# Norm factors by Ln and Exp on ScalarE, and the group norm's sums of squares placed behind the memory value tiles

## What is computed

```python
def rms_norm(x, g):
    xf = x.astype(jnp.float32)
    y = xf * lax.rsqrt(jnp.mean(xf * xf, axis=-1, keepdims=True) + RMS_EPS)
    return (y * g.astype(jnp.float32)).astype(x.dtype)
...
    # in rwkv7_mixer, after the recurrence; H = 16 heads of N = 64 channels
    mean = jnp.mean(y, axis=-1, keepdims=True)
    var = jnp.mean(jnp.square(y - mean), axis=-1, keepdims=True)
    yn = ((y - mean) * lax.rsqrt(var + RWKV_GN_EPS)).reshape(B, S, D)
    yn = yn * gn_g.astype(jnp.float32) + gn_b.astype(jnp.float32)
...
    out = (yn + bonus.reshape(B, S, D)).astype(x.dtype)
    return (out * g) @ w_o
```

## Time and profile before

| | |
|---|---|
| three runs | 3185.61, 3197.8, 3207.39 us; median 3197.8 |
| the profiled execution | 3202.03 us, of which span 3200.0 |
| mean granted clock of PE in it | 0.97 of full speed |
| PE busy | 3048.5 us, 16020 matmul records |
| DVE busy | 1005.6 us |
| ACT busy | 1026.7 us |
| POOL busy | 789.7 us |

### The profile page before, as it was taken

How to read it: one execution, slowest core, us unless ns; L and a number is a source line. 1 busy time by engine, 2 the same in 40 slices (tenths; PEclk the granted TensorE clock), 3 DMA queues, 4 the chain that set the end, 5 groups by cost and what they waited for, 6 DMA issues and landing times.

```text
span 3200.0 us, 37773 instructions
## 1 busy us (share of the span) xinstructions
PE 3048.5 (95%) x16020; PEld 2148.2 (67%) x16020; DVE 1005.6 (31%) x1552; ACT 1026.7 (32%) x1630; POOL 789.7 (25%) x399
## 2 busy tenths in 40 slices
PE   8999999999987999899999999998999999999996
PEld 6687778885675787577788777776887473333332
DVE  5444330115587743632411224144120330000001
ACT  4543442334662222243433324413221131111111
POOL 3122244441330000032344432200442121111110
PEclk9999999999898799999999999999999999999998
DMA  3242122230220002221232232110332249999996
GB/s 126 89 138 73 53 91 94 92 105 22 94 68 1 2 2 80 86 79 61 85 105 92 92 95 90 53 53 1 98 100 73 88 187 400 399 400 399 399 394 244
DMA packets 214262, 416.41 MB, mean 130 GB/s; under 512 B 18486, under 2 KB 195670, under 8 KB 201168
## 3 DMA queue, kind: packets, MB, share of 16 engines
q1 hardware_dynamic: 199248, 394.30, 33.8%
q0 software_dynamic: 14704, 19.70, 1.8%
q10 hardware_dynamic: 144, 0.01, 0.0%
HBM read 501.70 MB, written 16.79 MB: 162 GB/s over the span
## 4 chain that ended last, share of the span: by engine, by line
PE 86%; DVE 7%; ACT 3%; DMA 2%; issue 1%; POOL 1%; SPq 0%; ACTq 0%; POOLq 0%; DVEq 0%
PE product_banks L600 15%; PE product_banks L602 14%; PE product_banks L601 14%; PE product_banks L2227 10%; PE product_banks L2264 5%; PE product_banks L568 5%; PE product_banks L695 3%; PE score_banks L1203 1%; PE stat_bank L823 1%; PE product_banks L1224 1%; PE product_banks L976 1%; PE product_banks L2820 1%; DVE SC L751 1%; PE product_banks L1590 1%; PE stat_bank L733 1%
## 5 line engine op out<-in xcount | busy, mean ns | idle before, releaser
L500 POOL TENSOR_TENSOR Wr_parts<-Wr,Wr_parts 128x1024 fp32r<-128x1024 f32 x202 | 488.6, 2420 | 1138.1 <-ACT Wr_parts L477 1138.1
L601 PE MATMUL product_banks<-A_parts,Wr_parts 128*128 128x512 f32 x1520 | 594.4, 391 | 0.0
L477 ACT ACTIVATE Wr_parts<-Wr 128x1024 fp32r<-128x1024 f32 x202 | 213.4, 1059 | 633.4 <-PE product_banks L602 586.9
L2227 PE MATMUL product_banks<-A,Wr 128*64 128x512 f32 x1312 | 340.5, 597 | 1.2 <-ACT Wr L2290 1.2
L600 PE MATMUL product_banks<-H_parts,Wr_parts 128*128 128x512 f32 x840 | 334.5, 398 | 3.0 <-POOL Wr_parts L500 2.5
L602 PE MATMUL product_banks<-H_parts,Wr_parts 128*128 128x512 f32 x840 | 329.0, 392 | 0.0
L601 PEld LDWEIGHTS product_banks<-A_parts,Wr_parts 128*128 128x128 f32 x1520 | 287.2, 189 | 59.8 <-issue 1.0
L500 POOL TENSOR_TENSOR shared_con_parts<-Wr,shared_con_parts 128x1024 fp32r<-128x1024 f32 x80 | 192.1, 2401 | 461.8 <-ACT shared_con_parts L477 461.8
L600 PE MATMUL product_banks<-A_parts,Wr_parts 128*128 128x512 f32 x680 | 267.2, 393 | 3.9 <-POOL Wr_parts L500 2.0
L602 PE MATMUL product_banks<-A_parts,Wr_parts 128*128 128x512 f32 x680 | 265.5, 390 | 0.0
L2227 PEld LDWEIGHTS product_banks<-A,Wr 128*64 128x64 f32 x1312 | 107.1, 138 | 209.9 <-issue 205.6
(11 more groups left out here) (529 smaller groups left out, 4753.4 us busy)
## 6 DMA issues: line engine op xcount, KB each, us to landing
A<-in_w_down SPq DMA_DIRECT2D x29, 2048.0 KB, 13.0
A<-in_w_gate SPq DMA_DIRECT2D x28, 2048.0 KB, 11.9
A<-in_w_up SPq DMA_DIRECT2D x28, 2048.0 KB, 15.7
Wr<-in_m_w_up SPq DMA_DIRECT2D x32, 1024.0 KB, 5.3
Wr<-in_m_w_down SPq DMA_DIRECT2D x32, 1024.0 KB, 5.0
Wr<-in_w_in SPq DMA_DIRECT2D x32, 1024.0 KB, 5.6
Wr<-in_c_w_kv SPq DMA_DIRECT2D x16, 1024.0 KB, 5.5
Wr<-in_b_w_rkv SPq DMA_DIRECT2D x12, 1024.0 KB, 5.0
```

The costliest lines, as they stand in the source:

```text
L477: nc.scalar.activation(weight_parts(s)[0], loaded_part(s), ACT.Copy).then_inc(*mark("weights_high", s))
L500: nc.gpsimd.tensor_tensor(lo, loaded_part(s), hi, ALU.subtract).then_inc(*mark("weights_split", s))
L601: pe.matmul(bank[:, :], hi[:, k, :], x_lo, start=False, stop=False)
L2227: mm = pe.matmul(BK[r, 0 if kind == "gate" else 1, :], XT[b % 2][:, k * P + CAP * h:k * P + CAP * h + CAP], unit_rows((kind, b, h))[:, k, ...
```

## The change

Both parts are in one diff. In `norm_root` ACT computes Ln(mean + eps) from the bank, waits for its own result, and then Exp(-0.5 times it) in place; `root_ready` now comes from the Ln and `rstd_ready` from the Exp, and DVE's reciprocal is gone from `norm_rstd`. For four of the 16 norms ACT is told ahead of its waits to load the set of tables that holds both Ln and Exp. The group norm gets the same pair in place of its root and reciprocal. Its sums of squares move on PE from in front of the memory values into them, one behind each value tile, the idle products between them go, and ACT takes value tile j just before factor j.

```diff
         def norm_root(act, n, tiles_=DT, width=T, dim=D, eps=EPS):
 
+            if n in ("l0n", "a0m", "l0o", "a1_m"):
+                nc.scalar.preload_act_table_set("natural_log_exp_and_others")
             act.wait_ge(*at("squares_summed", (n, tiles_ - 1)))
             if norms_before(n):
                 act.wait_ge(*at("norm_applied", norms_before(n)[0]))
-            nc.scalar.activation(RS[:, 0:width], B7[:, 0:width], ACT.Sqrt, scale=1.0 / dim,
+            nc.scalar.activation(RS[:, 0:width], B7[:, 0:width], ACT.Ln, scale=1.0 / dim,
                                  bias=eps_col(eps)).then_inc(*mark("root_ready", n))
+            act.wait_ge(*at("root_ready", n))
+            nc.scalar.activation(RS[:, 0:width], RS[:, 0:width], ACT.Exp, scale=-0.5).then_inc(
+                *mark("rstd_ready", n))
 
         def norm_rstd(dve, n, width=T):
 
-            dve.wait_ge(*at("root_ready", n))
-            nc.vector.reciprocal(RS[:, 0:width], RS[:, 0:width]).then_inc(*mark("rstd_ready", n))
             dve.wait_ge(*at("rstd_ready", n))
...
-        def values_pe(pe, tag):
+        def values_pe(pe, tag, **kw):
             product_rows(pe, tag + "v", lambda k, m: memory(tag, k)[:, m * P:(m + 1) * P],
-                         lambda k: [])
+                         lambda k: [], **kw)
...
             gn_act(act)
-            for j in range(8):
-                take_value(act, "a1_", j)
             first_highs(act, "w_o")
...
             keys_pe(pe, "a1_")
-            for j in range(8):
+
+            def square_sum(j):
                 pe.wait_ge(*at("y_square", j))
                 pe.wait_ge(*at("y_centred", 7))
                 if j >= 2:
                     pe.wait_ge(*at("y_root", j - 2))
                 pe.matmul((B6, B7)[j % 2][:, :], cc("blk"), SQ[:, j % 2, :], start=True,
                           stop=True).then_inc(*mark("y_square_summed", j))
-                if j % 2:
-                    idle_products(pe, 4, S2[:, 0, :])
-            values_pe(pe, "a1_")
+
+            values_pe(pe, "a1_", then=square_sum)
             product(pe, "g2", lambda k: LB[:, 1, :], lambda k: [])
...
             for j in range(8):
-                if 1 <= j < 7:
-                    square(j + 1)
+                take_value(act, "a1_", j)
                 act.wait_ge(*at("y_square_summed", j))
                 if j >= 2:
                     act.wait_ge(*at("y_normed", j - 2))
-                nc.scalar.activation(TMP[:, j % 2, :], (B6, B7)[j % 2][:, :], ACT.Sqrt,
-                                     scale=1.0 / HD, bias=eps_col(GN_EPS)).then_inc(
-                    *mark("y_root", j))
+                s = TMP[:, j % 2, :]
+                alink(act, nc.scalar.activation(s, (B6, B7)[j % 2][:, :], ACT.Ln,
+                                                scale=1.0 / HD, bias=eps_col(GN_EPS)))
+                nc.scalar.activation(s, s, ACT.Exp, scale=-0.5).then_inc(*mark("y_root", j))
+                if j < 6:
+                    square(j + 2)
...
             for j in range(8):
                 dve.wait_ge(*at("y_root", j))
                 s, y = TMP[:, j % 2, :], tile(Y0 + j)
-                link(dve, nc.vector.reciprocal(s, s))
```

## The result

The changed kernel took 3156.9 us (median of 7; 3153.6 to 3167.7), the kernel before, run beside it, 3185.6 (median of 7; 3181.8 to 3207.4): a ratio of 0.9894, 95% interval 0.9873 to 0.9916. A second comparison on another chip gave 3158.5 against 3188.1, ratio 0.9911 (0.9881 to 0.9942). So the gain is 28.7 and 28.4 us by medians, 33.8 was forecast. The intervals of the two ratios reach from 27 to 40 us and from 18 to 38, so by the times alone the forecast is not excluded; what it had wrong shows by stages. The profiled execution has a span of 3155.1 us at a mean granted clock of 0.976, against 3200.0 at 0.970.

What follows compares the result with a forecast made beforehand. PE was taken to bound the chain (86%), so only its idle time could be gained: 5.9 + 5.3 + 1.3 + 22.5 - 1.2 = 33.8 us, from a median of 3197.8 to 3164, range 3152 to 3180.

Steps and rivals of the forecast that it cites:

- Group norm, 22.5: Eight rounds interleaved with value tiles at PE's pace, 4.32 us each, without PE waits; w_o's weights 22.5 us earlier.
- the tail: Behind the group norm's values: DVE's g2 multiplication waits to about 4.0 us, covered by 1.6; uncovered it costs up to 3.
- m0x and l1n, 5.3: Two norms one behind the other: ACT's copies of mixes start 2.65 + 2.70 us earlier, gain 5.3, lower bound 3.5.
- a1_m, 1.3: Norm with the reciprocal on the chain: gain 1.3 us, limited by a PE product that ends at 1238.9.
- The rival: Clock rival: less idling avoids some clock falls, at 1242 and 1345, each worth 1.5 to 3 us; about 3160, chance 0.10.
- The branch norms, 5.9: At l0o, a0x, l1o, a1x the high part comes 2.7 us earlier; PE gains its idle time, 1.14 + 1.81 + 1.13 + 1.81.
- the forecast's own sign of being wrong: The forecast is wrong if the idle products turn out not to bind at the branch norms.
- The key root, -1.2: At L1318 after cn, a new load for Sqrt of 1.28 us delays the root and weight copies: 1.2 us lost.
- The other norms, 0: l0n, a0n, m0n, a1_n, m1n, a0m, cm, m1x, cn: covered by PE's other work, so gain 0.
- The clock: PE's granted clock, 1.0 or 0.5: falls at 1242 and 1345 might not come, each worth 1.5 to 3 us; chance 0.10.
- The pin: Naming the set at four norms suffices; rival: each Ln and Exp loads, gain only 16.5 us, 3181, chance 0.06.
- The case that it held for the likelier: Faster by over 1%, 32 us, chance 0.54, against same 0.43 and slower 0.03; the forecast of 33.8 was just above it.

Runs made afterwards that it cites:

- e3: Changed kernel with POOL's weight copy ahead of Ln and the branch's last scaled copy behind Exp at four branch norms: 3156.7 us, ratio 0.9875; again 3157.2, 0.9868.
- e8: Kernel before, with only POOL's weight copy moved ahead of the root at the four branch norms: PE idle 1.14 us at l0o, 2.18 instead of 1.81 at a0x.
- e7: Changed kernel with the group norm's sums of squares and their idle products back in front of the values: 3179.8 us, ratio 0.9943 to before.
- e2: Kernel before with only the group norm's sums of squares moved behind the value tiles, root and reciprocal kept: 3183.2 us, ratio 0.9946.
- e6: Changed kernel without the two lines of norm_root that name the set of tables: 3175.2 us, ratio 0.9946 to before.
- e5: e3 without the nine idle products behind the sums of l0o, a0x, l1o and a1x: 3165.8 us, ratio 0.9932 to before.

## Why the prediction was right or wrong

- **Group norm, 22.5.** Measured 22.5. The round (4.31 for 4.32), the absence of waits and the tail all held: DVE's first g2 multiplication came 3.9 us after the last value tile for the 4.0 forecast, and w_o's first product 13.6 after it, as before. It is the term that carried the forecast.
- **m0x and l1n, 5.3.** Measured 5.4, the root of l1n 2.7 earlier (766.40 for 769.14) for the 2.65 counted through. Taking the ACT chain and not PE's first product (3.7 by the traces) was right.
- **a1_m, 1.3.** The events came 1.3 earlier; PE still idled 2.0 us, the clock fell all the same and stayed low longer into L3384, which took 0.9 back. The rival had hoped for a gain there.
- **The branch norms, 5.9: wrong, 2.9.** The step that failed is the one that has "the high part comes 2.7 us earlier" and PE's idle time gone at all four places. It takes DVE's scale and residual at the length that they had before. Of the weight copy at l0o the text asks when POOL's low part is ready for PE ("just in time", and so it was), not what DVE does beside POOL meanwhile. Before, the reciprocal lay over the whole L500 (252.34 to 255.69 against 253.34 to 255.69); with it gone the L500 stands under the scales and the first residual, which takes 2.84 for 0.68, and PE idled for 1.33 us at l0o and 0.56 at the others. That is the forecast's own sign of being wrong: the idle products did not bind. e3 shows the cause by moving the L500, e8 that its place is no matter with the reciprocal there. With the collision gone the idle products bind, as the text had it, but the four places then gain 6.9 by PE's rows and not 5.9: the idle times of 1.14 and 1.81 stand for 1.4 and 2.05 of delay.
- **The key root, -1.2.** Measured -1.3 at the root and at PE's next product, -0.8 a few us on, when the clock had come back: the load takes 1.28 and the root stands right behind it. The 2.6 that the Trainium skill's drain behind a load would have made (ScalarE: Activation LUTs, "What ACT_TABLE_LOAD costs") did not show.
- **The other norms, 0.** No PE wait appeared at any of them; a shift of 0.8 us near l0n in the changed kernel's first trace is 0.0 in e7's, with the same norms, and 1.1 in e2's, with the old ones, so it is no cost of the change.
- **The clock.** The falls forecast as avoidable at 1242 and behind g2 came all the same. The 16.6 us in the first pair of profiles (8.1 and 8.5) came from two stretches, one of which the prediction had read the earlier trace rows as a fixed part of the kernel; they differ from one execution to the next.
- **The pin.** It holds where it is placed, and e6 shows that it is needed; the rival took 17.3 us off the gain (33.8 to 16.5), 1.8 times too much.
- **The number.** 3164 against 3156.9 is two errors that partly cancel, so that the time fell into the range is in part luck: the kernel before has a median of 3185.6 in seven runs where three had given 3197.8 (12.2 lower), and the gain is 28.7 by medians instead of 33.8, 30.4 by the rows. The text priced the spread of three runs at 5. The case that it held for the likelier, faster by over 1% (0.54), rested on a gain just above 32 us; with the branch norms' missing 3.0 it is gone. The ratios are 0.9894 and 0.9911, with intervals to 0.9916 and 0.9942: neither is shown to be faster by over 1%.

## What to carry to other kernels

When an instruction goes, look at what ran beside it on the engine that can lock its own out: here a reciprocal with one SBUF operand was a harmless neighbour of POOL's subtraction, and the two-operand products that moved into its place were not. Where a helper's work can be issued earlier, move it under the time in which the other engine waits anyway. And where the clock varies from one execution to the next, compare kernels at equal clock loss, and stage by stage, before a difference of two profiles is called a gain; the fit alone misjudged a stage here in which PE waited at a low clock.

## What the runs showed of the hardware

- A DVE `tensor_tensor` with two SBUF inputs took 2.84 us instead of 0.68 beside a POOL `tensor_tensor` of 2.51 us and ended 0.55 behind it; a reciprocal (3.35) and a multiplication with one input in PSUM (0.68) were not held; POOL's took 2.80 instead of 2.36 where DVE's was first.
- Without its set named, the compiled program loads a table at every change between Ln and Exp: 47 loads of 1.283 us where 4 do.
- The time lost to PE's granted clock explains nearly all of the spread between executions of one kernel: 0.83 us per us lost, with 1.7 us left over, where the times themselves lie 15 to 30 us apart.
- Behind 4.84 us of idling the products ran at a granted clock of 0.50 (256 to 260 us in e5, 0.63 us each); with constants on PE in that time they ran at 1.00 (0.39 us).
- Products that follow one another directly overlap in the profile, so an idle time of 0.56 us in front of one stood for 0.81 of delay.
